# First mixer of a decoder trunk: transposed input, stationary dt weights, running sums spread through device memory

## The chip, the cores and the metric

One core of a Trainium2 chip runs the whole program. The metric is the device time of one launch in microseconds (us). A core has a matrix engine (PE, with its weight loads as PEld), a vector engine (DVE), a scalar engine (ACT), GpSimd (POOL) and a sync engine (SP) that here issues the transfers; 16 DMA engines move the data. Everything is float32.

## The reference

The trunk has two layers: a Mamba-2 layer (here the first mixer, `mixer_a`) with a mixture of experts behind it, and a sliding-window attention layer with a second mixture of experts. The change touches the first mixer only:

```
proj = rms_norm(h, norm_w) @ in_w                      # h: 256 tokens x 1024
z, xbc, dt, q_mem = split(proj)                        # xbc: 2560 channels, dt: 24 heads
xbc = silu(causal_depthwise_conv(xbc, conv_w, conv_b)) # width 4
dt  = softplus(dt + dt_bias); a = -exp(a_log)
# per chunk of 128 tokens:
acum  = cumsum(dt * a)                                 # running sums, one row per head
decay = exp(where(causal, acum[l] - acum[s], -inf))
y = ((C B^T) * decay) @ (x * dt) + (C @ state) * exp(acum) + d_skip * x
y = group_rms_norm(y * silu(z)) * gnorm_w
out = concat(y, memory_cross_attention(q_mem)) @ out_w
```

`decay` needs, for each of 24 heads and 2 chunks, the running sum as a row over l, the same on all 128 partitions, minus the running sum as a column over s.

## The kernel before

All tensors lie with 128 partitions. The work of the mixer is cut into units of PE; each writes one of eight PSUM banks in turn. One list, `order` in `mixer_a`, sets the order of the units, and PE, ACT and DVE each walk the same list: PE makes the unit's matmuls, ACT or DVE evict it and do what follows. So each engine meets the units in the same order, and an engine that waits at one unit holds up everything of its own behind it. PE needs a bank to be freed before it writes it (`U.wait_free`).

The units around the change: `xT` 0 to 3 are transposes of the normed input (ACT evicts them into `xnT`, scaled with `a_norm`), `dt` is the projection to 24 heads, `conv` 0 to 19 are the projections to the 2560 channels (8 matmuls of 128x256 each), whose four taps DVE adds up (L1027, L1029) and ACT passes through silu (L774). DVE makes softplus of dt in a chain of 17 small operations at its place behind `dt`. Then `z`, transposes of xs and B (`xtok`, `bt`), the cumulated sums as columns (`ac`), the norm and transposes of the memory tokens (`memT`).

Then come eight steps (2 chunks times 4 groups), which I number 0 to 7, with a ninth round, 8, for the last products. Step i holds `cb` i (scores C B^T), the two units `A` 2i and 2i+1 (L923: for three heads each, PE multiplies a head's column of dt*a, spread over 128 columns, with the triangle `tri`, which leaves the running sum as a row on all partitions), some units of the memory attention (`between`: `q`, `mk`, `mv`, `sc`, `pT`, `pv`), then `st` or `yo` and `yd` of step i-1. At `A`, DVE subtracts the column (L1053) into the buffer `E[i % 4]`, ACT takes exp (L799), and DVE multiplies with the scores (`decay_scores`, one `A` unit late). `yd` of step i multiplies `E` with x*dt; only after it may `E` be written again, two steps later.

SP issues all transfers on one queue in the order in which they are needed: the input x in two halves, the table `small` (constants and small weights), the weight tiles of the mixer (2 MB each, in two halves of 1 MB, in 11 slots of their own, each refilled when its tile is used), then the first 17 MB of expert weights into slots as they come free. The expert stages behind the mixer use the same slots.

Of the kernel before, what the change touches and what calls it, by code (L numbers as in the profile page):

```python
# [22 lines left out]
F32 = mybir.dt.float32  # L23
# [24 lines left out]
NEG = -1e30  # L48
GRAN = 2048
# [563 lines left out]
def mixer_a(c):  # L613
# [5 lines left out]
             "out_tile mem1_dve " + Router.SEMS)  # L619
    s = c.sems("mixer", names)  # L620
    ld_small = c.sem("ld_small")
    ld_x, ld_mem = ([c.sem(f"ld_{n}{t}") for t in range(NT)] for n in ("x", "mem"))
    with ctx:
# [13 lines left out]
        cbm = [sb(f"cbm{i}", P) for i in range(2)]  # L637
        xw = [acc[:, i * GW:(i + 1) * GW] for i in range(2)]
        sq = xw

# [27 lines left out]

        def freed(kind, i):
# [13 lines left out]
        U = Units(c, order, freed, holds)  # L683
# [18 lines left out]
        x_norm = Norm(c, c.h, 0, s["x_act"], s["x_dve"])  # L702
# [1255 lines left out]
```

## Time and profile before

| | us |
|---|---|
| median of 3 runs | 1407.54 (1406.74 to 1410.73) |
| profiled execution | 1409.6 |
| its span, first to last instruction | 1407.8 |
| PE busy in the span | 1217.6 (86%) |
| DVE, ACT, POOL busy | 271.9, 205.7, 33.5 |
| moved by DMA | 458.76 MB, mean 326 GB/s |

The span is 1.8 us shorter than the profiled execution, and that is 2.1 us above the median. The profile cuts the span in 40 slices of 35.2 us; the mixer takes the first eight, the experts of the first layer come next.

### The profile page before, as it was taken

The numbers are of one execution on the slowest core, as the hardware profiler recorded it, in microseconds if no ns is written. First come the engines' busy times: TensorE is split into PE (matmuls) and PEld (weight loads), VectorE is DVE, ScalarE is ACT, GpSimd is POOL, SyncE is SP. The second block draws the span as 40 slices with busy tenths as digits, with TensorE's granted clock in tenths as the row PEclk, the third lists the DMA queues.
The fourth block names the chain that finished last, engine by engine and source line by source line (L and its number), as shares of the span: only waits on it lengthen the run. The fifth ranks groups of instructions, "written<-read, shape, count | busy, mean of one in ns | idle before, by whom it ended". The sixth has DMA issues, their size and how long they took to land. (4 is left out here: it accounts for less than half of the span.)

```text
span 1407.8 us, 15101 instructions
## 1 busy us (share of the span) xinstructions
PE 1217.6 (86%) x6038; PEld 616.4 (44%) x6038; DVE 271.9 (19%) x679; ACT 205.7 (15%) x490; POOL 33.5 (2%) x42
## 2 busy tenths in 40 slices
PE   6999999989999999659666998989999999657654
PEld 6875875444444445223212566454444444212211
DVE  3541552131111110000001156031101101000001
ACT  3124232110000000000002146130000000000001
POOL 0001210000000000000000011000000000000000
PEclk9999999989999999889887999989999999887877
DMA  9543307559999998999999612549999999999993
GB/s 381 192 144 120 120 0 288 198 234 424 422 423 424 423 424 329 426 420 427 423 425 357 262 60 91 209 139 420 422 423 425 425 424 424 426 423 427 423 424 163
DMA packets 94665, 458.76 MB, mean 326 GB/s; under 512 B 7040, under 2 KB 7040, under 8 KB 61696
## 3 DMA queue, kind: packets, MB, share of 16 engines
q1 hardware_dynamic: 94592, 457.75, 79.7%
q8 instruction: 51, 0.84, 0.2%
q14 instruction: 22, 0.18, 0.0%
HBM read 456.67 MB, written 1.05 MB: 325 GB/s over the span
## 5 line engine op out<-in xcount | busy, mean ns | idle before, releaser
L1395 PE MATMUL bank<-own,e_xg 128*64 128x512 f32 (+1 forms) x1312 | 280.2, 667 | 40.2 <-DMA own<-in_w_up 18.3
L1395 PE MATMUL bank<-late,e_xg 128*64 128x512 f32 (+1 forms) x736 | 177.3, 652 | 35.1 <-DMA own<-in_w_up 19.9
L1404 PE MATMUL bank<-own,e_turned 128*32 128x512 f32 (+1 forms) x656 | 145.9, 704 | 49.2 <-DMA own<-in_w_down 35.6
L1395 PEld LDWEIGHTS bank<-own,e_xg 128*64 128x64 f32 (+1 forms) x1312 | 81.1, 134 | 198.8 <-issue 198.5
L1287 DVE TENSOR_TENSOR e_hid<-e_silu,bank 128x512 f32<-128x512 f32 x24 | 16.5, 688 | 509.7 <-ACT e_silu L1338 509.7
L1395 PEld LDWEIGHTS bank<-late,e_xg 128*64 128x64 f32 (+1 forms) x736 | 50.6, 132 | 129.3 <-issue 129.3
L1370 PEld LDWEIGHTS bank<-e_pick,xs 128*128 128x128 f32 x768 | 94.4, 201 | 20.5 <-issue 18.2
L1370 PE MATMUL bank<-e_pick,xs 128*128 128x128 f32 x768 | 100.9, 288 | 2.1 <-DVE e_pick L1234 2.1
L1404 PE MATMUL bank<-late,e_turned 128*64 128x512 f32 (+1 forms) x368 | 87.5, 673 | 16.7 <-DMA own<-in_w_down 6.3
L1404 PEld LDWEIGHTS bank<-own,e_turned 128*32 128x32 f32 (+1 forms) x656 | 41.0, 139 | 128.0 <-issue 118.4
L1338 ACT ACTIVATE e_silu<-bank 128x512 f32<-128x512 f32 x24 | 14.3, 597 | 548.1 <-PE bank L1395 548.1
L1387 PE MATMUL bank<-e_y,e_gates_T 128*128 128x512 f32 x192 | 86.5, 593 | 1.4 <-ACT e_gates_T L1346 1.4
L394 PE MATMUL bank<-a_xnT,own 128*128 128x256 f32 x384 | 85.3, 384 | 0.0
L394 PEld LDWEIGHTS bank<-a_xnT,own 128*128 128x128 f32 x384 | 73.9, 193 | 10.2
L1292 DVE COPY e_y<-bank 128x512 f32<-128x512 f32 x24 | 16.6, 692 | 256.6 <-PE bank L1404 256.6
L1387 PEld LDWEIGHTS bank<-e_y,e_gates_T 128*128 128x128 f32 x192 | 34.6, 190 | 36.3 <-issue 34.4
L1404 PEld LDWEIGHTS bank<-late,e_turned 128*64 128x64 f32 (+1 forms) x368 | 24.5, 137 | 58.8 <-issue 50.8
L1344 ACT ACTIVATE e_y<-bank 128x512 f32<-128x512 f32 x24 | 14.3, 597 | 244.9 <-PE bank L1404 244.9
L1245 DVE TENSOR_TENSOR e_xg<-bank,small 128x512 f32<-128x512 f32 x48 | 33.2, 692 | 57.8 <-PE bank L1370 57.8
L394 PE MATMUL bank<-own,a_xnT 128*128 128x512 f32 x96 | 42.1, 593 | 0.0
L377 PE MATMUL bank<-own,a_xbcT 128*128 128x512 f32 x96 | 41.8, 593 | 0.0
L394 PE MATMUL bank<-own,b_xnT 128*128 128x512 f32 x64 | 30.6, 636 | 1.1 <-ACT b_xnT L1616 1.1
(326 smaller groups left out, 997.9 us busy)
## 6 DMA issues: line engine op xcount, KB each, us to landing
own<-in_w_up SPq DMA_DIRECT2D x83, 1024.0 KB, 12.0
own<-in_w_down SPq DMA_DIRECT2D x82, 1024.0 KB, 12.5
own<-in_w_gate SPq DMA_DIRECT2D x81, 1024.0 KB, 13.3
late<-in_w_gate SPq DMA_DIRECT2D x47, 1024.0 KB, 13.8
late<-in_w_down SPq DMA_DIRECT2D x46, 1024.0 KB, 12.2
late<-in_w_up SPq DMA_DIRECT2D x45, 1024.0 KB, 11.9
own<-in_a_in_w SPq DMA_DIRECT2D x18, 1024.0 KB, 11.8
own<-in_mem_w_kv SPq DMA_DIRECT2D x8, 1024.0 KB, 9.4
```

The lines of the kernel that those rows point to most:

```text
L377: ins = pe.matmul(U.bank(("out", 2 * t + half))[:, :], src(t, 4 * (m - n) + j), c.rows_at(m, j)[:, 512 * half:512 * half + 512], start=Fal ...
L394: ins = pe.matmul(out, lhsT(k), rhs(k), start=(k == 0), stop=(k == n - 1))
L1245: dve.tensor_tensor(cut(self.xg[:, 512 * half:512 * half + 512], k=4), cut(bank, k=4), spread_last(c.f(f"ffn_norm{layer}", 4 * half, 4 * h ...
L1287: dve.tensor_tensor(self.hid[:, :], self.silu[:, :], self.b_up[:, :], ALU.mult).then_inc(s["hid_ready"], 1)
L1292: dve.tensor_copy(self.y[1][:, :], self.b_down[1][:, :]).then_inc(s["y_ready"], 1)
L1338: act.activation(self.silu[:, :], self.b_gate[:, :], ACT.Silu).then_inc(s["silu_done"], 1)
L1344: act.activation(self.y[0][:, :], self.b_down[0][:, :], ACT.Copy).then_inc(s["y_ready"], 1)
L1370: ins = pe.matmul(bank[:, k * P:(k + 1) * P], xs[:, t, 4 * half + k, :], cut(self.pick, t=NT)[:, t, :], start=(t == 0), stop=(t == NT - 1))
L1387: ins = pe.matmul(self.sums[2 * t + out][:, :], self.gates_T[:, t * P:(t + 1) * P], self.y[out][:, :], start=first, stop=last, skip_group_ ...
L1395: ins = pe.matmul(bank[q * T:(q + 1) * T, :], self.xg[:, at:at + T], cut(tile(q), k=4)[:, k, :], start=(half == 0 and k == 0), stop=(half ...
L1404: ins = pe.matmul(self.b_down[out][q * T:(q + 1) * T, :], self.turned[:, at:at + T], cut(tile(q), j=2)[:, j, 512 * out:512 * out + 512], s ...
```

## The change

- The host also passes x transposed, as `xT` (128 x 2048). SP loads the first 564 columns of `small` (`FIRST_FIELDS`), the halves of `xT` and of weight tile 0 in turn, the rest of `small`, tiles 1 to 4, the memory tokens, and only then x itself.
- The `xT` units are gone. ACT scales `xT` with `a_norm` into `xTw`, DVE squares it, and a new unit `ss` (8 matmuls with `ones` as weights) leaves the sum of squares of each token on all partitions. `norm_x` turns that into `rb`, 1 over the norm, and `xnT` = `xTw` * `rb`.
- `conv` 0 to 3 multiply with the unnormed `xTw`; DVE multiplies their result with `rb` into `raw` before the taps, so they take 5 DVE operations and not 4.
- `dt` is split: `dtp` has the dt weights stationary, 32 columns, in four column groups of the array; ACT copies it to `dtT`; `dt` adds the four groups with two matmuls.
- The `A` units have no PE work. A new unit `acT` makes the running sums as 48 rows, ACT copies them and stores them in device memory (`acum_rows`), and `load_decays` on ACT loads each buffer `E` with three rows broadcast to 128 partitions: for steps 0 and 1 behind `memT`, for step i+2 when PE has done `yd` of step i.

```diff
-        order = [("xT", i) for i in range(4)] + [("dt", 0)]
-        order += [("conv", j) for j in range(NCONV)]
-        order += [("z", 0), ("xtok", 0), ("xtok", 1), ("xtok", 2), ("bt", 0), ("ac", 0), ("z", 1), ("xtok", 3), ("xtok", 4), ("xtok", 5)]
+        order = [("conv", 0), ("conv", 1), ("ss", 0), ("conv", 2), ("conv", 3), ("dtp", 0), ("conv", 4), ("dt", 0)]
+        order += [("conv", j) for j in range(5, NCONV)]
+        order += [("z", 0), ("xtok", 0), ("xtok", 1), ("xtok", 2), ("bt", 0), ("ac", 0), ("acT", 0), ("z", 1), ("xtok", 3), ("xtok", 4), ("xtok", 5)]
...
         @block.sync
         def _(sp):
-            for t in range(NT):
-                sp.dma_start(cut(c.h, t=NT)[:, t, :], g["x"][0, t * P:(t + 1) * P, :]).then_inc(ld_x[t], 16)
-            sp.dma_start(c.small[:, :], g["small"]).then_inc(ld_small, 16)
-            for n in range(2):
+            sp.dma_start(c.small[:, 0:FIRST_SMALL], g["small"][:, 0:FIRST_SMALL]).then_inc(ld_first, 16)
+            for half in range(2):
+                at = slice(4 * half * SEQ, 4 * (half + 1) * SEQ)
+                sp.dma_start(xT[:, at], g["xT"][:, at]).then_inc(ld_xT[half], 16)
+                c.load_mixer_half(sp, 0, half)
+            sp.dma_start(c.small[:, FIRST_SMALL:], g["small"][:, FIRST_SMALL:]).then_inc(ld_small, 16)
+            for n in range(1, 5):
                 c.load_mixer_tile(sp, n)
...
+            for k in range(KD):
+                act.wait_ge(ld_xT[k // 4], 16)
+                act.activation(cut(xTw, k=KD)[:, k, :], cut(xT, k=KD)[:, k, :], ACT.Copy, scale=c.f("a_norm", k, k + 1)).then_inc(s["xw_ev"], 1)
+            act.wait_ge(s["rb_dve"], 1)
+            act.activation(rb[:, :], rb[:, :], ACT.Sqrt).then_inc(s["rb_act"], 1)
+
+            def load_decays(st):
+                for i in (2 * st, 2 * st + 1):
+                    ch, gr = steps[st]
+                    row = SSD_HEADS * ch + HG * gr + 3 * (i % 2)
+                    rows = acum_rows[row:row + 3, :].rearrange("(o r) l -> o (r l)", o=1)
+                    act.dma_start(E[i % 4][:, :], rows.broadcast_to([P, GW])).then_inc(e_loaded[i % 4], 16)
...
+                if kind == "dtp":
+                    U.wait_done(act, key)
+                    act.activation(dtT, bank[:, 0:SEQ], ACT.Copy).then_inc(s["dtp_ev"], 1)
+                    act.wait_ge(ld_small, 16)
+                elif kind == "acT":
+                    U.wait_done(act, key)
+                    act.activation(acT, bank[0:NT * SSD_HEADS, 0:P], ACT.Copy).then_inc(s["acT_ev"], 1)
+                    act.wait_ge(s["acT_ev"], 1)
+                    act.dma_start(acum_rows, acT).then_inc(s["acum_stored"], 16)
...
+                    if i == 3:
+                        act.wait_ge(s["acum_stored"], 16)
+                        for st in range(2):
+                            load_decays(st)
...
+                elif kind == "yd" and i < 6:
+                    U.wait_done(act, key)
+                    load_decays(i + 2)
...
+                elif kind == "ss":
+                    pe.wait_ge(s["sq_dve"], 2)
+                    project(c, pe, out[:, 0:256], lambda k: c.f("ones"), lambda k: cut(squares, k=KD)[:, k, :])
...
+                elif kind == "dtp":
+                    pe.wait_ge(s["xn_dve"], 2)
+                    for k in range(KD):
+                        q = DT_ROWS * (k % 4)
+                        ins = pe.matmul(out[q:q + DT_ROWS, 0:SEQ], cut(c.f("dt_w"), k=KD)[:, k, :], cut(xnT, k=KD)[:, k, :],
+                                        start=(k < 4), stop=(k >= 4))
+                    ins.then_inc(c.units_done, 1)
                 elif kind == "dt":
-                    pe.wait_ge(s["xT_ev"], 8)
+                    pe.wait_ge(s["dtp_ev"], 1)
...
+                elif kind == "acT":
+                    pe.matmul(out[0:NT * SSD_HEADS, 0:P], adt[:, :], c.f("tri"), start=True, stop=True).then_inc(c.units_done, 1)
-                elif kind == "A":
-                    ch, gr = steps[i // 2]
-                    for hh in range(3):
-                        hd = HG * gr + 3 * (i % 2) + hh
-                        ins = pe.matmul(out[:, hh * P:(hh + 1) * P], cut(adt, t=NT)[:, ch, hd:hd + 1].broadcast_to([P, P]),
-                                        c.f("tri"), start=True, stop=True)
-                    ins.then_inc(c.units_done, 1)
...
+            def norm_x():
+                U.wait_done(dve, ("ss", 0))
+                dve.tensor_scalar(rb[:, :], U.bank(("ss", 0))[:, 0:SEQ], 1.0 / D, EPS, ALU.mult, ALU.add).then_inc(s["rb_dve"], 1)
+                dve.wait_ge(s["rb_act"], 1)
+                dve.reciprocal(rb[:, :], rb[:, :]).then_inc(s["rb_dve"], 1)
+                dve.wait_ge(s["rb_dve"], 2)
+                dve.wait_ge(s["xw_ev"], KD)
+                for half in range(2):
+                    k = slice(4 * half, 4 * half + 4)
+                    dve.tensor_tensor(cut(xnT, k=KD)[:, k, :], cut(xTw[:, :], k=KD)[:, k, :], spread_mid(rb[:, :], 4), ALU.mult).then_inc(s["xn_dve"], 1)
...
+                    if i < 4:
+                        step(dve.tensor_tensor(raw[i], bank[:, 0:SEQ], rb[:, :], ALU.mult))
+                        bank = raw[i]
...
-                    U.wait_done(dve, key)
-                    if i >= 4:
-                        dve.wait_ge(c.units_done, U.at["yd", (i - 4) // 2] + 1)
+                    dve.wait_ge(e_loaded[i % 4], 16 * (i // 4 + 1))
```

How the instructions stand, in three places. First PE's queue from the start to the first z unit, before (`xs` is the normed input, `own` a weight slot):

```order
L333 MATMUL bank<-small,xs 128x128 x16
L885 MATMUL bank<-small,a_xnT 128x24 x16
L394 MATMUL bank<-a_xnT,own 128x256 x160
L394 MATMUL bank<-own,a_xnT 128x512 x8
L333 MATMUL bank<-small,a_xbcT 128x128 x16
```

and after (`xs` now holds `xTw`; L936 is `dtp`, L942 is `dt`):

```order
L922 MATMUL bank<-xs,own 128x256 x8
L396 MATMUL bank<-xs,own 128x256 x8
L396 MATMUL bank<-a_xbcT,small 128x256 x8
L396 MATMUL bank<-xs,own 128x256 x16
L936 MATMUL bank<-a_xnT,small 32x256 x8
L396 MATMUL bank<-a_xnT,own 128x256 x8
L942 MATMUL bank<-small,a_xbcT 128x24 x2
L396 MATMUL bank<-a_xnT,own 128x256 x120
```

The transposes and the 16 dt matmuls ahead of the projections are gone; five conv units, `ss` and `dtp` stand ahead of `dt`, and fifteen conv units stand behind it.

Second, ACT's queue at the same place, before (L766 evicts the transposes, L770 is the exp of dt, L774 the silu of the conv units):

```order
L766 ACTIVATE a_xnT<-bank,small 128x256 x8
L770 ACT_TABLE_LOAD
L770 ACTIVATE a_dt<-a_dt 128x48
L771 ACTIVATE a_ea<-small 128x24
L774 ACT_TABLE_LOAD
L774 ACTIVATE a_xbcT<-a_acc 128x256 x20
```

and after, with what each waits for (L815 is now the silu, L790 the copy of `dtp` to `dtT`, L811 the exp of dt):

```order
L756 ACTIVATE xs<-memT,small 128x256 [waits ld_xT0] x4
L756 ACTIVATE xs<-memT,small 128x256 [waits ld_xT1] x4
L758 ACTIVATE a_cbm<-a_cbm 128x256 [waits mixer_rb_dve]
L815 ACT_TABLE_LOAD
L815 ACTIVATE a_xbcT<-a_acc 128x256 [waits mixer_conv_dve] x4
L790 ACTIVATE a_xbcT<-bank 128x256 [waits units_done]
L815 ACTIVATE a_xbcT<-a_acc 128x256 [waits mixer_conv_dve,ld_small]
L811 ACT_TABLE_LOAD
L811 ACTIVATE a_dt<-a_dt 128x48 [waits mixer_dt_dve]
```

The copy L790 stands behind the silu of conv 0 to 3, and each of those waits for DVE.

Third, PE in step 7, before (L917 is `cb`, L923 the two `A` units, L394 is `mk` 1, L349 `pv` 0, L341 `sc` 1, L943 `yo`, L949 `yd` 6):

```order
L917 MATMUL bank<-a_xbcT 128x128
L923 MATMUL bank<-small,a_dt 128x128 x6
L394 MATMUL bank<-late,own 128x256 x8
L349 MATMUL bank<-a_xbcT,late 128x256 x2
L341 MATMUL bank<-late,a_qT 128x256 x2
L943 MATMUL bank<-a_xbcT 128x384
L949 MATMUL bank<-late,xs 128x64 x6
```

and ACT from there on after the change (L767 are the two loads for step 7, behind `yd` 5; L840 the exps of `A` 14 and 15; L834 the eviction of `mk` 1, L856 that of `pv` 0, L848 the exps of `sc` 1):

```order
L767 DMA xs<-acum_rows 128x384 [waits units_done]
L767 DMA xs<-acum_rows 128x384
L840 ACTIVATE xs<-xs 128x384 [waits mixer_seg_dve] x2
L834 ACTIVATE late<-bank 128x256 [waits units_done]
L856 ACTIVATE a_qT<-bank 128x256 [waits units_done]
L848 ACTIVATE a_xbcT,a_smc<-bank,a_smc 128x256 [waits mixer_sm_max,units_done]
```

PE's row L923 is gone from each of the eight steps, and two transfers stand on ACT ahead of the exps of steps 2 to 7.

## Rows read from the trace of the kernel before

**Rows 1.** The page: busy share of the DMA engines, in tenths, 40 slices.

```profile
DMA  9543307559999998999999612549999999999993
```

**Rows 2.** Waits of PE, 0 to 240 us: total, times, longest.

```profile
PE bank L333 <- DVE xs L422: 10.9, 1, 10.9
```

**Rows 3.** Waits of PE, 290 to 700 us, the longest group.

```profile
PE bank L1404 <- DMA own<-in_w_down: 19.9, 4, 6.3
```

**Rows 4.** Timeline of the start: start us, length, what, count, idle and releaser.

```profile
0.75 0.87 SPq L712 DMA_DIRECT2D h<-in_x  x2
...
4.63 1.06 ACT L412 ACTIVATE xs<-h 128x1024 f32<-128x1024 f32 x1 [2.60 <-DMA h<-in_x]
...
8.45 0.88 POOL L468 TENSOR_TENSOR small<-small 128x288 f32<-128x288 f32 x1 [8.00 <-DMA small<-in_small]
...
10.87 3.65 PE L333 MATMUL bank<-small,xs 128*128 128x128 f32 x16 [10.87 <-DVE xs L422]
...
15.44 7.02 PE L885 MATMUL bank<-small,a_xnT 128*128 128x24 f32 x32 [0.93 <-ACT a_xnT L766]
...
22.29 37.94 PE L394 MATMUL bank<-a_xnT,own 128*128 128x256 f32 x167
```

**Rows 5.** Timeline of PE: the first z unit, behind conv 19.

```profile
93.09 7.03 PE L394 MATMUL bank<-own,a_xnT 128*128 128x512 f32 x16
```

**Rows 6.** Timeline of DVE and ACT: conv 0 and the start of conv 1.

```profile
27.75 0.54 DVE L1027 TENSOR_SCALAR a_acc<-bank,small 128x256 f32<-128x256 f32 x1 [0.51 <-PE bank L394]
28.33 1.52 DVE L1029 SCALAR_TENSOR_TENSOR a_acc<-bank,small,a_acc 128x255 f32<-128x255 f32 x3
29.88 0.42 ACT L774 ACTIVATE a_xbcT<-a_acc 128x256 f32<-128x256 f32 x1 [5.24 <-DVE a_acc L1029]
31.20 0.54 DVE L1027 TENSOR_SCALAR a_acc<-bank,small 128x256 f32<-128x256 f32 x1 [1.36 <-PE bank L394]
```

**Rows 7.** DVE operations of other widths: a timeline row, then groups by form.

```profile
23.67 0.45 DVE L1010 RECIPROCAL a_dt<-a_dt 128x48 f32<-128x48 f32 x1
...
L1089 DVE TENSOR_TENSOR late<-late,xs 128x384 f32<-128x384 f32 x8 | 4.5, 558 | 0.3
L1073 DVE TENSOR_TENSOR a_xbcT<-a_xbcT,a_smc 128x512 f32<-128x512 f32 x4 | 2.8, 692 | 0.1
L997 DVE TENSOR_SCALAR late<-late,a_gss 128x384 f32<-128x384 f32 x8 | 2.7, 416 | 0.0
```

**Rows 8.** Timeline of PE around the A units of step 0.

```profile
133.12 1.50 PE L923 MATMUL bank<-small,a_dt 128*128 128x128 f32 x12
134.46 7.03 PE L394 MATMUL bank<-own,a_xnT 128*128 128x512 f32 x16
```

**Rows 9.** Timeline of PE around a wait in the experts (32-column weights, four column groups).

```profile
562.51 3.64 PE L1404 MATMUL bank<-own,e_turned 128*32 128x512 f32 x32 [0.47 <-ACT e_turned L1341]
572.16 5.12 PE L1404 MATMUL bank<-own,e_turned 128*32 128x512 f32 x32 [6.01 <-DMA own<-in_w_down]
```

**Rows 10.** Windows there: length, busy (count) of PE, PEld, DVE, ACT, POOL, PEclk, DMA share, GB/s.

```profile
568.00:570.00 2.00, 0.00 (x0) 0.00 (x0) 0.00 (x0) 0.00 (x0) 0.00 (x0) 0.59 1.03 424
...
574.00:576.00 2.00, 2.00 (x20) 0.55 (x16) 0.00 (x0) 0.00 (x0) 0.00 (x0) 0.70 1.08 451
576.00:578.00 2.00, 2.00 (x19) 0.93 (x12) 0.66 (x1) 0.66 (x2) 0.00 (x0) 1.00 0.96 397
```

**Rows 11.** Step 7, from the timelines of PE, DVE and ACT: yd 5; A 14; eviction of mk 1; sc 1.

```profile
193.58 1.45 PE L949 MATMUL bank<-late,xs 128*128 128x64 f32 x12
...
197.11 0.86 DVE L1053 TENSOR_SCALAR xs<-bank,a_acum 128x128 f32<-128x128 f32 x3
...
200.14 0.38 ACT L793 ACTIVATE late<-bank 128x256 f32<-128x256 f32 x1
...
200.80 1.03 PE L341 MATMUL bank<-late,a_qT 128*128 128x256 f32 x4
```

**Rows 12.** Line L248 (SP's 1 MB loads), 60 to 80 us: issue to landing.

```profile
DMA to landing us min/median/max: 4.7/5.9/7.4
```

**Rows 13.** Line L394 of PE, 23 to 24 us: count, busy, mean ns.

```profile
L394 PE MATMUL bank<-a_xnT,own 128*128 128x256 f32 x4 | 2.1, 669 | 0.0
```

More of the change, by code:

```diff
@@ L636, in mixer_a @@
         yt = c.xs[:, 4 * GW:5 * GW]
[L637 removed]
+        cbm2 = sb("cbm", 2 * P)
+        cbm = [cbm2[:, P * i:P * i + P] for i in range(2)]
         xw = [acc[:, i * GW:(i + 1) * GW] for i in range(2)]
         sq = xw
+        xT, xTw, rb = c.memT1, c.xs, cbm2
+        squares, raw, dtT = xbcT[:, 8 * SEQ:16 * SEQ], [xbcT[:, (16 + i) * SEQ:(17 + i) * SEQ] for i in range(4)], xbcT[:, 15 * SEQ:16 * SEQ]
+        acT = qT[0:NT * SSD_HEADS, 0:P]
         state, ex, pTs = xbcT[:, 0:4 * GW], [xbcT[:, 4 * GW + 512 * i:4 * GW + 512 * i + 512] for i in range(2)], xbcT[:, 4 * GW + 1024:4 * GW + 1536]
@@ L681, in freed @@
                     "out": (s["h_new"], i + 1)}[kind]
-        U = Units(c, order, freed, holds)
+        pe_order = [key for key in order if key[0] != "A"]
+        U = Units(c, pe_order, freed, holds)
         R = Router(c, U, s, 0, xnT, acc)
@@ L717, in _ @@
                 sp.dma_start(cut(mem, t=NT)[:, t, :], g["mem"][0, t * P:(t + 1) * P, :]).then_inc(ld_mem[t], 16)
-            for n in range(2, TILES_A):
+            for t in range(NT):
+                sp.dma_start(cut(c.h, t=NT)[:, t, :], g["x"][0, t * P:(t + 1) * P, :]).then_inc(ld_x[t], 16)
+            for n in range(5, TILES_A):
                 for half in range(2):
@@ L733, in _ @@
         def _(act):
-            for t in range(NT):
-                act.wait_ge(ld_x[t], 16)
-                x_norm.act(act, t)
+            act.wait_ge(ld_first, 16)
+            act.activation(c.norm_r[:, 6:7], c.f("ones", 0, 1), ACT.Sqrt)
+            for k in range(KD):
[9 more added lines that the diff above has]
+                    act.dma_start(E[i % 4][:, :], rows.broadcast_to([P, GW])).then_inc(e_loaded[i % 4], 16)
             for key in order:
@@ L863, in _ @@
         def _(pe):
-            for key in order:
+            pe.wait_ge(ld_first, 16)
+            for key in pe_order:
                 kind, i = key
@@ L871, in _ @@
                     U.wait_free(pe, key)
-                if kind == "xT":
-                    if i == 0:
-                        pe.wait_ge(ld_small, 16)
-                        pe.wait_ge(s["x_dve"], 6)
-                    norm_T_units(c, pe, out, i)
+                if key == ("conv", 0):
+                    for k in range(KD):
+                        if k % 4 == 0:
+                            c.wait_job(pe, ("mixer", 0, k // 4))
+                        pe.wait_ge(s["xw_ev"], k + 1)
+                        ins = pe.matmul(out[:, 0:256], c.cols_at(0, k)[:, 0:P], cut(xTw, k=KD)[:, k, :], start=(k == 0), stop=(k == KD - 1))
+                    ins.then_inc(c.units_done, 1)
+                elif kind == "ss":
+                    pe.wait_ge(s["sq_dve"], 2)
+                    project(c, pe, out[:, 0:256], lambda k: c.f("ones"), lambda k: cut(squares, k=KD)[:, k, :])
                 elif kind == "memT":
@@ L972, in chain @@
                 return step
-            for t in range(NT):
-                x_norm.dve(dve, t)
+            for half in range(2):
+                at = slice(4 * half * SEQ, 4 * (half + 1) * SEQ)
+                dve.wait_ge(ld_xT[half], 16)
+                dve.tensor_tensor(squares[:, at], xT[:, at], xT[:, at], ALU.mult).then_inc(s["sq_dve"], 1)
+            dve.wait_ge(ld_first, 16)
+            def norm_x():
[5 more added lines that the diff above has]
+                dve.wait_ge(s["xw_ev"], KD)
+                for half in range(2):
+                    k = slice(4 * half, 4 * half + 4)
+                    dve.tensor_tensor(cut(xnT, k=KD)[:, k, :], cut(xTw[:, :], k=KD)[:, k, :], spread_mid(rb[:, :], 4), ALU.mult).then_inc(s["xn_dve"], 1)
+            norm_x()
             y_step = chain(s["y_dve"])
@@ L1021, in _ @@
                 elif kind == "conv":
-                    step = chain(s["conv_dve"], 4 * i)
+                    step = chain(s["conv_dve"], conv_done(i))
                     U.wait_done(dve, key)
+                    if i == 4:
+                        dve.wait_ge(ld_small, 16)
                     if i >= 3:
```

69 lines of the change are left out of this document (39 added, 30 removed).

## The prediction

> **What bounds the kernel now.** I read the page's slices first. The DMA engines are at 8 or 9 tenths from the tenth slice on, but for five slices in the middle; in the eight slices of the mixer they are at 9, 5, 4, 3, 3, 0, 7 and 5 [rows 1]. So the experts are bound by their weights, the mixer is not. The waits of PE come next. In the first 240 us PE waits once for long, 10.9 us at the very start, for the normed input [rows 2]; from there it works without a gap to the router. Later the waits are for weights, such as 19.9 us for w_down in 290 to 700 us [rows 3]. A stage bound by PE and one bound by DMA behind it add up: the stream of expert weights cannot run ahead of the mixer, because the 17 slots hold it. So each us that the mixer gets shorter should come off the time whole, and I work out only by how much PE reaches its router sooner. What ends last there is PE's own queue, and it is walked strictly in order.
>
> **Start of the projections.** Before, PE starts at 10.87 us, runs 16 transposes and the dt matmuls, and reaches conv 0 at 22.29 [rows 4] and the first z unit at 93.09 [rows 5]. A conv unit takes 3.45 us at full pace (27.75 to 31.20 [rows 6]); 20 of them are 69.1 us of the 70.8. The other 1.7 us are matmuls at half pace: mean 669 ns and four in 23 to 24 us [rows 13].
>
> When do the new inputs land? Two halves of x and `small` (2.11 MB) are there at 8.45 us, the first half of x (0.52 MB) at 4.63 [rows 4]: a stream of 0.41 MB/us that starts at 3.3 us. The new order gives: first table 4.0, `xT` half 5.3, weights half 7.8, second `xT` 9.1, second weights 11.7. ACT scales a quarter of a half in about 0.42 us (the 128x256 activation [rows 6]) and is ready before each half of the weights.
>
> Conv 0 then starts at 7.9. Its first eight instructions run at half pace, 3.4 us, the rest at 11.75. After the pause in the experts the granted clock was 0.50 to 575.2 us (0.70 in 574 to 576) and 1.00 from there, 3.0 us after the restart at 572.16 [rows 9, 10], so I take 1.2 GHz to 11 and 2.4 GHz behind: conv 0 ends at 13.5 (15.2 if all of it is slow). Conv 1 ends at 17.0, `ss` at 20.4, conv 2 and 3 at 27.3. `dtp`: 32 instructions with 32-column weights and 512 columns take 3.64 us [rows 9], so 16 with 256 columns take 0.9; end 28.2. Conv 4 ends at 31.6. [...]
>
> **The new wait.** `dt` needs ACT's copy of `dtp`, which stands on ACT behind the silu of conv 0 to 3, and these wait for DVE. DVE begins when `ss` is done, 20.8 with 0.4 of latency: 0.54 (the 256-wide operation [rows 6]); ACT's root 0.42; the reciprocal of 256, from 0.45 for 48 [rows 7] with 0.15 of it taken as fixed and the rest scaled, 1.75 (bounds 1.2, and 2.4 if all of it scales); two multiplications of 1024, from 0.56 for 384 and 0.69 for 512 [rows 7], 1.22 each. With gaps that is 26.1. Then four conv units: 0.43 for the new multiplication (between 0.3 and 0.56), 0.35 for the first tap, which now reads SBUF (2.7 us for eight of 384 [rows 7], bound 0.54), 1.52 for the rest, 0.1 of gaps: 2.4 each, 35.7. Silu and copy 0.42 each: `dt` on PE at 36.6, where PE has stood since 31.6. Behind it on PE stand all fifteen conv units. `dt` takes 0.45, the fifteen 51.8, and the clock will have dropped in these 5 us: in the experts' pause of 6.0 us the clock was 0.59 in the window that begins 1.9 us into it, and came back 3.0 us after the restart [rows 9, 10]. That costs 1.6 us. The z unit starts at 37.05 + 51.8 + 1.6 = 90.5 and not 93.1: **-2.6 us**. The head start of 9 us is mostly given back. Bounds: -4.7 (DVE 0.5 sooner, clock kept) and +1 (all of conv 0 slow, first tap 0.54, reciprocal 2.4). DVE then catches up, at 2.1 us a unit against 3.45 [rows 6]. The dt chain of 17 operations hides as before.
>
> **The A units.** From 133.12 to 134.46 PE spends 1.34 us on them [rows 8], eight times: -10.7. `acT` is one such matmul of 128 columns, +0.2. **-10.5 us**. Its copy and store on ACT, the first four loads and their landing lie ahead of step 0 by two z units of 7.03 us each [rows 5] and cost nothing; with that cover gone they would cost one landing.
>
> **The new transfers.** From step 2 on a load may be issued only when `yd` of two steps before is done, at time T on PE. The row of PE's own unit is replaced by: ACT sees the end and issues (0.3), landing L. For L the nearest row is 4.7 us for 1 MB [rows 12], of which 2.6 are its bytes at 0.41 MB/us: 2.1 fixed, plus 0.5 for 0.2 MB, plus 0.6 for sharing with a weight tile that SP loads just then: 3.3 from the issue (bounds 2.5 and the row's own maximum, 7.4). Behind the waiting operation on DVE stand three subtractions (0.86 [rows 11]) and the multiplication with the scores (0.55), which PE's `yd` needs: ready at T + 0.3 + L + 1.4. PE has `cb` 0.27, the units between and 0.64 for `st` to do meanwhile. With one 3.45 us unit between (steps 2 and 4) it is there at T + 4.4 and stands 0.6 us each time; with seven us between (3, 5, 6) it never waits. Step 7 is worse. There `sc` 1 needs `mk` 1 evicted, and ACT does that behind the exps of A 14 and 15. Before: T = 193.58 + 1.29 = 194.87; DVE starts A 14 at 197.11, `mk` 1 is evicted at 200.52, `sc` 1 starts at 200.80 [rows 11]. So the path through DVE and ACT is 5.65 us long and hides PE's A units already. Without them PE comes to `sc` 1 at T + 4.6, and the path, begun at T + 0.3 + L = T + 3.6 and 3.4 long, ends at T + 7.0: 2.4 us. Together 3.6, with 0.4 for the weight tile that is in flight at step 2: **+4.0 us** (bounds 1.7 at L = 2.5, 12 at L = 6).
>
> ACT also waits at each `yd` now. What stands behind that are exps, which could not run sooner either, since their buffer is only free then.
>
> By the Trainium skill (DMA: Bandwidth & Descriptors, Anatomy of one DMA) such a transfer takes 2.0 us and bytes / 436e9, an estimate of 2.45 here; no run here shows one of this size yet. With it the stalls would sum to about 1.6 and the time to some 1396. It also says (Issuing engines are not separate DMA queues) that ACT's transfers interleave with SP's on the same 16 engines, which speaks against the change.
>
> **Sum.** -2.6 - 10.5 + 4.0 = -9.1 us. The profiled span of 1407.8 would become 1398.7, and the median of 1407.5 becomes 1398.4. The profiled execution lies 2.1 above the median, within the spread of 4 us of the three runs.
>
> **Rivals.**
> (a) More gain, under 1394. DVE needs less for the SBUF operations, so `dt` comes by 35 and the wait is short enough for the clock, and loads land in 2.5 us: -4.7 - 10.5 + 1.7 = -13.5, 1394. Against it: both must hold.
> (b) The transfers eat the gain. Stalls by L: steps 2 and 4 L - 2.7 each, step 7 L - 0.9, steps 3, 5, 6 from about 6.2, 7.1 and 6.7. At L = 5 they sum to 8.7, at 6 to 11.7: 1403 to 1406. For it: the tile in flight at steps 2 and 4, and a median of 5.9 us for loads that come in pairs [rows 12]. Against it: ACT's load is a fifth of such a one in bytes.
> (c) Slower. The same mechanism in steps 2 to 7: it loses from L = 6.4 (stalls 13.1) and by more than 4.2 us from L = 7.3. That is so when the broadcast of one row to 128 partitions, or a queue behind SP's tiles, makes the landing as late as 7.4 [rows 12]. Then 2 x 4.7 + 6.5 + 1.2 + 0.3 + 0.7 = 18.1, less 13.1: +5, 1412.5.
> (d) The head start is lost altogether: conv 0 slow throughout and DVE at its upper bounds, +1 for the start. That alone gives 1402.
>
> **Chances.** The forecast, with (d) in it, 1394 to 1403.3: 0.68. (a) 0.11. (b) 0.16. (c) 0.05. A difference of 0.3%, 4.2 us, is about what a measurement of this kernel can tell from none. Faster by more than that: 0.68 + 0.11 = 0.79; within it 0.16, slower 0.05. For the range I go down to 1392.5, half of (a), and up to 1405, part of (b).
>
> **What would show it.** PE's conv 0 in two pieces, from 7.9 and 11.75. A wait of PE for ACT's copy (L790) of about 5 us, with the clock at half for some 3 us behind it. The z unit at 90.5. No long PE wait at steps 3, 5, 6; about 0.6 at 2 and 4, and 2.4 at `sc` 1. ACT's loads landing in some 3.3 us. The router reached 9 us sooner and the rest shifted whole. It would be wrong if the loads take 5 us or more, if DVE's start path is shorter than 26.1 or if the DMA-bound part does not shift along.

## The result and the profile after

The changed kernel takes 1415.84 us (median of 6 runs, 1415.0 to 1418.34) against 1407.6 (6 runs, 1405.24 to 1410.73) before: a ratio of 1.0059, 95% interval 1.0044 to 1.0074. It is slower by 8 us where I forecast 9 us faster. The profiled execution took 1415.68 us with a span of 1413.8, against 1407.8.

The page's rows of the DMA engines come first, as in [rows 1]; under each row of shares stands the row of GB/s. After:

```profile
DMA  9643408569999999999998612559999999999994
GB/s 357 243 145 142 164 23 330 197 247 418 418 417 416 415 416 367 422 409 421 414 418 339 237 60 90 208 191 417 416 417 418 417 418 415 420 415 421 414 418 168
```

and before:

```profile
GB/s 381 192 144 120 120 0 288 198 234 424 422 423 424 423 424 329 426 420 427 423 425 357 262 60 91 209 139 420 422 423 425 425 424 424 426 423 427 423 424 163
```

The shares say the same in both kernels, 9 tenths wherever the experts stream their weights. The GB/s don't: 420 to 425 before in most of those slices, 414 to 418 after. Equally busy engines moved 1.6% less. This is in code that the diff doesn't touch. My rows had the shares alone, and these can't show it.

Waits of PE in 0 to 240 us after, which answer to [rows 2], with total, times and longest:

```profile
PE bank L922 <- DMA own<-in_a_in_w: 9.5, 2, 9.3
PE bank L942 <- ACT a_xbcT L790: 4.1, 1, 4.1
PE bank L1002 <- issue: 3.6, 2, 3.4
PE bank L343 <- ACT late L834: 1.2, 1, 1.2
```

The first is the start (10.9 before). The others are the three new stalls: `dt` for the copy of `dtp`, `yd` of step 3, and `sc` 1 for the eviction of `mk` 1.

Timeline of PE at the start, which answers to [rows 4, 5]:

```profile
9.28 3.75 PE L922 MATMUL bank<-xs,own 128*128 128x256 f32 x8 [9.28 <-DMA own<-in_a_in_w]
13.22 2.22 PE L922 MATMUL bank<-xs,own 128*128 128x256 f32 x8 [0.19 <-DMA own<-in_a_in_w]
...
29.18 1.07 PE L936 MATMUL bank<-a_xnT,small 128*32 128x256 f32 x16
30.18 3.72 PE L396 MATMUL bank<-a_xnT,own 128*128 128x256 f32 x16
38.03 1.04 PE L942 MATMUL bank<-small,a_xbcT 128*128 128x24 f32 x4 [4.13 <-ACT a_xbcT L790]
38.91 54.77 PE L396 MATMUL bank<-a_xnT,own 128*128 128x256 f32 x240
...
93.51 7.03 PE L396 MATMUL bank<-own,a_xnT 128*128 128x512 f32 x16
```

Both halves of conv 0 wait for weights; `dt` starts at 38.03 after a wait of 4.13 us; the first z unit is at 93.51, no sooner than the 93.09 of [rows 5].

Steps 3 and 4, timelines of PE, ACT's queue and DVE (L767 are the two loads for step 4, L1127 the subtraction on `A` 8, L1052 the product for `A` 7, L1002 `yd` 3):

```profile
160.00 0.88 SPq L250 DMA_DIRECT2D own<-in_a_out_w  x2
...
161.93 0.82 ACTq L767 DMA_DIRECT2D xs<-acum_rows  x2
...
168.39 0.68 DVE L1127 TENSOR_SCALAR xs<-xs,a_acum 128x128 f32<-128x128 f32 x3 [4.98 <-DMA xs<-acum_rows]
168.99 0.55 DVE L1052 TENSOR_TENSOR xs<-xs,a_cbm 128x384 f32<-128x384 f32 x1
...
169.64 1.80 PE L1002 MATMUL bank<-late,xs 128*128 128x64 f32 x12 [3.37 <-issue]
...
171.76 8.22 PE L396 MATMUL bank<-own,late 128*128 128x512 f32 x16
```

Two weight halves were issued by SP at 160.00, and the loads at 161.93 land behind them: DVE gets `A` 8 at 168.39. PE stands at `yd` 3 because DVE makes the product of `A` 7 only behind the subtraction on `A` 8. Then `mv` 0 takes 8.22 us and not 7.03. The landings of all 16 loads, minimum, median and maximum:

```profile
DMA to landing us min/median/max: 2.9/3.3/6.4
```

Step 7, which answers to [rows 11]:

```profile
195.86 1.03 PE L351 MATMUL bank<-a_xbcT,late 128*128 128x256 f32 x4
198.10 1.10 PE L343 MATMUL bank<-late,a_qT 128*128 128x256 f32 x4 [1.22 <-ACT late L834]
```

PE has four milestones in every one of these kernels: the first z unit, the gather of the router's picks, the first expert matmul, the end of the span. The last two columns were read from the program, not the trace: where slot 0 of the weight slots (`own`) starts in SBUF in each partition, and what is left of that over a multiple of 256 bytes.

| kernel | z | gather | experts | span | experts to end | GB/s, 1000 to 1200 us | start of `own` | over 256 |
|---|---|---|---|---|---|---|---|---|
| before | 93.09 | 289.92 | 296.23 | 1407.8 | 1111.6 | 424 | 42240 | 0 |
| after | 93.51 | 287.31 | 292.44 | 1413.8 | 1121.4 | 417 | 42592 | 96 |
| e5_aligned | 92.47 | 287.84 | 293.31 | 1404.9 | 1111.6 | 423 | 42752 | 0 |
| e6_shifted | 91.46 | 288.30 | 294.86 | 1417.5 | 1122.6 | 417 | 42592 | 96 |
| e9_off128 | 91.26 | 288.11 | 294.69 | 1417.7 | 1123.0 | 417 | 42368 | 128 |
| e10_off32 | 91.26 | 288.10 | 294.79 | 1420.5 | 1125.7 | 416 | 42272 | 32 |
| e3_start_only | 92.89 | 289.74 | 296.15 | 1418.5 | 1122.4 | 416 to 417 | 42592 | 96 |
| e4_sp_queue | 93.94 | 283.03 | 288.88 | 1411.1 | 1122.2 | 417 | 42592 | 96 |
| e7_start_aligned | 92.01 | 288.86 | 295.53 | 1404.6 | 1109.1 | 424 | 42752 | 0 |
| e11_copy_early | 85.97 | 282.80 | 288.73 | 1400.2 | 1111.5 | 424 | 42752 | 0 |
| e12_act_moves | 85.06 | 277.73 | 283.37 | 1397.5 | 1114.1 | 424 | 42752 | 0 |
| e8_best | 86.02 | 274.44 | 279.60 | 1391.0 | 1111.4 | 424 | 42752 | 0 |

Each slot is 8192 bytes in a partition, 32 times 256, so all 17 slots share the remainder in the last column. From the first expert matmul to the end the changed kernel takes 9.8 us more than before, and that is its whole loss: it gets there 3.8 us sooner.

### The profile page after: what moved, and what is told of

It reads as the page before. It is cut to its first block and busy times, and to the rows that moved or that the text cites. A ratio compares the mean times of both kernels' runs of the same rounds, so it can differ in the third digit from the quotient of the medians.

```text
span 1413.8 us, 14909 instructions
## 1 busy us (share of the span) xinstructions
PE 1213.5 (86%) x5932; PEld 600.7 (42%) x5932; DVE 272.5 (19%) x683; ACT 203.5 (14%) x488; POOL 32.7 (2%) x42
## 5 line engine op out<-in xcount | busy, mean ns | idle before, releaser
L1469 PE MATMUL bank<-own,e_xg 128*64 128x512 f32 (+1 forms) x1312 | 283.1, 674 | 36.3 <-DMA own<-in_w_up 16.8
L1478 PE MATMUL bank<-late,e_turned 128*64 128x512 f32 (+1 forms) x368 | 91.3, 696 | 19.9 <-DMA own<-in_w_down 11.0
L396 PE MATMUL bank<-a_xnT,own 128*128 128x256 f32 x320 | 72.8, 390 | 0.0
L396 PEld LDWEIGHTS bank<-a_xnT,own 128*128 128x128 f32 x320 | 62.4, 196 | 9.2 <-issue 0.4
```

The lines of the kernel that those rows point to most:

```text
L396: ins = pe.matmul(out, lhsT(k), rhs(k), start=(k == 0), stop=(k == n - 1))
L1469: ins = pe.matmul(bank[q * T:(q + 1) * T, :], self.xg[:, at:at + T], cut(tile(q), k=4)[:, k, :], start=(half == 0 and k == 0), stop=(half ...
L1478: ins = pe.matmul(self.b_down[out][q * T:(q + 1) * T, :], self.turned[:, at:at + T], cut(tile(q), j=2)[:, j, 512 * out:512 * out + 512], s ...
```

## Experiments: is it the queue or the tensors?

My first two suspects for the slower stream were parts of the change that last beyond the mixer: a second engine's DMA queue in use, and the new tensors. Each was put alone into the kernel before.

**e1_act_ring.** ScalarE issues one transfer of 4 KB.

```diff
+            act.dma_start(spare[:, :], g["small"][:, 0:8]).then_inc(extra, 16)
+            act.wait_ge(extra, 16)
```

> The kernel before, and one transfer of 4 KB issued by ACT at the very start. Nothing else is changed. In the changed kernel the weight stream of the experts ran at 416 to 418 GB/s and not at 423 to 425, in the whole expert stages. If a second transfer queue (ACT's) is what slows it (theory R), the stream falls to about 417 GB/s here too and the time rises by 8 to 12 us. If the layout of the tensors in device memory does it (theory T), the stream stays at 424 and the time within 2 us of before.

Measured 1409.76 us (10 runs), ratio 1.0008 (0.9995 to 1.002). The stream stays at 422 to 424 GB/s. The use of ACT's queue isn't it.

**e2_tensors.** The kernel before also loads `xT` and stores 48 rows to `acum_rows`, both by SP.

```diff
+            sp.dma_start(c.memT1[:, :], g["xT"]).then_inc(ld_xT, 16)
+            sp.dma_start(acum_rows, c.small[0:NT * SSD_HEADS, 0:P]).then_inc(stored_rows, 16)
```

> The kernel before, with the two tensors of the change in device memory: xT is loaded once (into the tile of the transposed memory tokens, which is overwritten later), and 48 rows are stored to acum_rows, both by SP; ACT issues nothing. Theory T: the stream falls to about 417 GB/s, time +8 to +12 us. Theory R: 424 GB/s and within 2 us of before.

Measured 1408.6 us (10 runs), ratio 1.0005 (0.9994 to 1.0017), stream 422 to 424 GB/s. Nor are the tensors in device memory.

**e3_start_only.** The changed kernel with the `A` units back on PE and without the transfers of running sums.

```diff
-        order += [..., ("ac", 0), ("acT", 0), ("z", 1), ...]
+        order += [..., ("ac", 0), ("z", 1), ...]
+                elif kind == "A":
...
-                    dve.wait_ge(e_loaded[i % 4], 16 * (i // 4 + 1))
+                    U.wait_done(dve, key)
```

> The changed kernel with the A units back on PE: no store, no loads by ACT, no acum_rows, but xT, the new start and dtp as changed. From the two traces the start alone gives the first z unit at 93.5 and not 93.1 us, so the mixer would be 0.4 us longer than before. Theory R: stream 424 GB/s, time 1408 (+0.4). Theory T, if xT does it: stream 417, time 1416 to 1420. If acum_rows does it: 424 as by R.

Measured 1419.52 us, ratio 1.007 (1.0053 to 1.0087), stream 416 to 417 GB/s: slower even than the changed kernel, with no transfer of its own left on ACT. So the loss is there without the running sums, and it isn't at the start either: z is at 92.89 and the gather at 289.74, both as before.

**e4_sp_queue.** The changed kernel with store and loads issued by SP, each at a fixed place in the list of weight tiles.

```diff
-                elif kind == "yd" and i < 6:
-                    U.wait_done(act, key)
-                    load_decays(i + 2)
...
+                for st in {(12, 1): (0,), (13, 1): (1, 2), (14, 1): (3, 4, 5)}.get((n, half), ()):
+                    sp.wait_ge(c.units_done, U.at["yd", st] + 1)
+                    load_decays(st + 2)
```

> The changed kernel with the store and the 16 loads issued by SP in place of ACT, and the weight tiles that were in flight at steps 2 and 4 issued behind them. Theory R: stream 424 GB/s, so the mixer's gain is left over: time 1402 to 1405. Theory T: stream 417, time 1412 to 1414. In either case PE's wait of 3.4 us in step 4 shrinks to under 1 us if it was the weight tile in flight that delayed the load, and the clock does not fall there.

Measured 1411.45 us (10 runs), ratio 1.0027 (1.0016 to 1.0038). The waits of PE in the mixer:

```profile
PE bank L925 <- DMA own<-in_a_in_w: 9.3, 2, 9.1
PE bank L945 <- ACT a_xbcT L802: 4.1, 1, 4.1
PE bank L343 <- ACT late L840: 1.3, 1, 1.3
PE bank L1005 <- issue: 0.5, 2, 0.3
```

The wait at `yd` falls from 3.6 to 0.5 us and half pace behind it goes. From z to the gather the kernel takes 189.09 us, after 193.80, before 196.83. The stream is still at 417 GB/s. The queue of the loads costs 4.4 us in the times, and the stream's loss is something else.

## Experiments: the place of the weights in SBUF

What the three kernels at 416 to 417 GB/s so far (the changed one, e3_start_only, e4_sp_queue) share is the table `small`, 8672 bytes per partition and not 8320. It stands ahead of the weight slots in SBUF and moves all of them: `own` starts at 42592, 96 bytes past a multiple of 256, and not at 42240, which is a multiple.

**e5_aligned.** The changed kernel and 40 unused columns in `small`, which bring `own` to 42752, a multiple of 256 again.

```diff
 FIRST_SMALL = sum(w for _, w in FIRST_FIELDS)
+FIELDS += [("pad", 40)]
```

> The changed kernel with 40 unused columns added to the table small, so that the weight slots behind it in SBUF start at a multiple of 256 bytes again (42752), as in the kernel before (42240); in the changed kernel they start at 42592, 96 bytes past one. Theory A (alignment of the weights' destination): the stream of expert weights returns to 424 GB/s and the 3.8 us by which the experts start sooner are left: 1403 to 1406. Theory S (something else in the new start, as the order or the split of the first transfers): stream 417, time 1415 to 1417.

**e6_shifted.** The kernel before and 88 unused columns, which put `own` exactly where the change puts it. Nothing else is changed.

```diff
-          ("dt_w", KD * SSD_HEADS)]
+          ("dt_w", KD * SSD_HEADS), ("pad", 88)]
```

> The kernel before with 88 unused columns added to small, which moves the slots by the same 352 bytes as the change does and changes nothing else but 45 KB more to load. Theory A: stream 417 GB/s, 1415 to 1420. Theory S: 424 GB/s, within 1.5 us of before.

e5_aligned takes 1405.45 us (9 runs), ratio 0.9975 (0.9964 to 0.9986); e6_shifted 1419.8 (6 runs), ratio 1.0077 (1.006 to 1.0094). Each way the step is 10 to 12 us. The stream in 1000 to 1200 us, first of the kernel before, then after, then e5_aligned, then e6_shifted:

```profile
DMA packets 14931, 84.77 MB, mean 424 GB/s; under 512 B 1293, under 2 KB 1293, under 8 KB 7891
```

```profile
DMA packets 14574, 83.44 MB, mean 417 GB/s; under 512 B 1268, under 2 KB 1268, under 8 KB 7527
```

```profile
DMA packets 15051, 84.67 MB, mean 423 GB/s; under 512 B 1291, under 2 KB 1291, under 8 KB 8156
```

```profile
DMA packets 14460, 83.49 MB, mean 417 GB/s; under 512 B 1271, under 2 KB 1271, under 8 KB 7282
```

The packets are of much the same size in all four, 5.6 to 5.8 KB on average; some 1.5% fewer bytes arrive in 200 us. Unused columns alone bring the loss and take it away, so it comes from where the length of `small` puts what lies behind it. Two things stay unseparated. The padding moves every tensor behind `small` in SBUF, the small ones too, though nearly all bytes of this stretch go into the weight slots. And it makes the table larger in device memory, so that the weights may start elsewhere there. No run moved the slots alone. Against the second: e2_tensors adds two tensors in device memory and stays at 424 GB/s in this stretch, and with `acum_rows` or without it the stream is at 417 (the changed kernel, e3_start_only) and at 423 to 424 (e5_aligned, e7_start_aligned).

**e9_off128 and e10_off32.** As e6_shifted with 32 and with 8 columns: 128 and 32 bytes past a multiple of 256.

```diff
-          ("dt_w", KD * SSD_HEADS)]
+          ("dt_w", KD * SSD_HEADS), ("pad", 32)]
```

```diff
-          ("dt_w", KD * SSD_HEADS)]
+          ("dt_w", KD * SSD_HEADS), ("pad", 8)]
```

> The kernel before with 32 unused columns more in the tile of small constants, so that every weight slot in SBUF starts 128 bytes past a multiple of 256 (own at 42368) instead of at one. Theory A in its first form (any start that is not a multiple of 256 costs): experts' stream 416 to 418 GB/s, 1417 to 1420 us. Theory A in its second form (only a start that is not a multiple of 128, or of 64, costs): 423 to 425 GB/s, 1406 to 1410 us. Rival (the number of columns or the size of the constants' load costs, not the address): in between, growing with the columns, about 1412.

> The kernel before with 8 unused columns more, so that every weight slot starts 32 bytes past a multiple of 256 (own at 42272). First form (any start that is not a multiple of 256 costs): 416 to 418 GB/s, 1417 to 1420 us. If only the distance counts, 32 bytes cost a third of what 96 do: about 1411. If 32 bytes is a fine start too: 423 to 425 GB/s, 1406 to 1410 us.

Measured 1419.98 us, ratio 1.0079 (1.0063 to 1.0094), at 417 GB/s, and 1423.0 us, ratio 1.0103 (1.0085 to 1.0121), at 416. So the first form holds at every distance tried: 32, 96 and 128 bytes cost 11 to 14 us. The number of columns doesn't decide it (8 cost the most), and the loss doesn't grow with the distance. The 1423.0 lies above the 1417 to 1420 of that form. All four runs at 32 bytes are slower than all four at 128 (1421.02 at least against 1420.79 at most), but the intervals of the ratios overlap, and why 32 should cost more stays open. 64 bytes wasn't tried, and both good starts, 42240 and 42752, are an odd multiple of 256; an even one wasn't tried either.

The Trainium skill (DMA: Bandwidth & Descriptors, How a descriptor splits into AXI transactions) says that a transaction has to start at a multiple of 256 bytes and that a descriptor that doesn't start at one fetches unused bytes from the boundary below. It says so of reading; that the same holds on the written side, here SBUF, is my extension of it. By that rule, the traces agree in sign and in that every remainder tried costs. An estimate from it is too high: with 83.44 MB in 14574 packets, 5.7 KB each, and a packet taken for a descriptor, one transaction more on 22 would be 4.5%, and the traces show 1.6%.

**e7_start_aligned.** e3_start_only with the 40 columns: what the new start is worth alone.

```diff
+FIELDS += [("pad", 40)]
```

> The new start alone (A units on PE, no transfers through device memory), with the slots at a multiple of 256 bytes. The start alone brought the first z unit to 92.9 us against 93.1. Theory A: 424 GB/s, 1407 to 1409. Theory S: 417, 1417 to 1420 as without the padding (1419.5).

Measured 1408.78 us (12 runs), ratio 0.9998 (0.9987 to 1.0008). The new start alone gives nothing. e5_aligned, with the running sums through device memory as well, is 3.3 us faster than this one.

## Experiments: the waits that were left

**e11_copy_early.** e7_start_aligned, and ACT copies `dtp` behind silu of conv 1.

```diff
+            act_order = [key for key in order if key not in (("dtp", 0),)]
+            act_order.insert(act_order.index(("conv", 1)) + 1, ("dtp", 0))
-            for key in order:
+            for key in act_order:
```

> The aligned kernel with the new start only (the e7 build: start changed, running sums still on TensorE) and one move on ScalarE: the copy of dt's projection goes behind silu of conv unit 1 instead of standing behind every conv unit. Theory: the 4.1 us wait of TensorE for that copy goes, and with it the 1.7 us by which the first in_z unit was slow behind it: 1408.8 less 6, 1402 to 1404 us, the first in_z unit at about 86 to 88. Rival (the wait passes to the next one late, the conv units or the own weights): 1406 to 1409.

Measured 1400.96 us (5 runs), ratio 0.9944 (0.993 to 0.9957). PE at the start, first of e7_start_aligned, then of e11_copy_early:

```profile
37.04 1.05 PE L920 MATMUL bank<-small,a_xbcT 128*128 128x24 f32 x4 [4.12 <-ACT a_xbcT L780]
37.91 54.26 PE L397 MATMUL bank<-a_xnT,own 128*128 128x256 f32 x240
...
92.01 4.46 PE L397 MATMUL bank<-own,a_xnT 128*128 128x512 f32 x10
```

```profile
33.72 0.52 PE L922 MATMUL bank<-small,a_xbcT 128*128 128x24 f32 x4
...
85.97 7.03 PE L397 MATMUL bank<-own,a_xnT 128*128 128x512 f32 x16
```

The wait is gone, not passed on, and `dt` takes half the time. The first z unit starts at 85.97, 6.0 us sooner, as expected; the median fell by 7.8, to 1400.96, which is 1 us below the lower end of the 1402 to 1404 expected. The start that gives nothing as the change has it (e7_start_aligned) is worth 7 to 8 us once one copy on ACT stands two units earlier.

**e12_act_moves.** e5_aligned with that move and with the eviction of `mk` 1 between the exps of `A` 14 and 15.

```diff
+            act_order = [key for key in order if key not in (("dtp", 0), ("mk", 1))]
+            act_order.insert(act_order.index(("conv", 1)) + 1, ("dtp", 0))
+            act_order.insert(act_order.index(("A", 14)) + 1, ("mk", 1))
```

> The changed kernel, aligned (the e5 build), with both moves on ScalarE (copy of dt's projection behind silu of conv unit 1; eviction of mask unit 1 between the exponentials of A14 and A15), the row stores and spread loads still on ScalarE's queue. By the sum 1405.5 less 4.1 and 1.7 (copy wait and half pace) less 1.2 (TensorE's wait for sc1): 1398 to 1399 us. It differs from e8 (1392.9) in the queue of the transfers alone: the theory that the loads on ScalarE's queue land late at step 4 puts 3 to 6 us between them, the rival (the queue is nothing, all of e8's gain is the moves) puts this one at 1393 to 1394.

**e8_best.** e4_sp_queue with the 40 columns and both moves. It differs from e12_act_moves in the queue of the transfers alone.

```diff
+FIELDS += [("pad", 40)]
...
+            act_order.insert(act_order.index(("conv", 1)) + 1, ("dtp", 0))
+            act_order.insert(act_order.index(("A", 14)) + 1, ("mk", 1))
```

> The changed kernel with slots at a multiple of 256 bytes, store and loads of the running sums issued by SP ahead of the weight tiles, and two moves in ACT's own order: the copy of dtp directly behind the silu of conv 1, and the eviction of mk 1 between the exps of A 14 and 15. Theory: PE's wait of 4.1 us for the copy and the half pace behind it (about 1.7) go, and the wait of 1.2 at sc 1. With theory A that is 1407.6 - 6.5 - 5.8 - 1.2 = 1394. If the copy is early but PE then waits for something later in the start (the taps on DVE, banks), the first z unit stays at 93 and the time at 1400. With theory S it would be 10 us more in either case.

e12_act_moves takes 1397.44 us (5 runs), ratio 0.9913 (0.9899 to 0.9927), 0.6 us under what was expected, and e8_best 1392.85 (5 runs), ratio 0.9885 (0.9869 to 0.99), 1.1 under. Waits of PE in the mixer of e12_act_moves and, below, of e8_best:

```profile
PE bank L1006 <- issue: 3.5, 2, 3.3
...
PE bank L344 <- ACT late L838: 0.2, 1, 0.2
```

```profile
PE bank L929 <- DMA own<-in_a_in_w: 8.6, 1, 8.6
PE bank L1009 <- issue: 1.0, 2, 0.7
PE bank L344 <- ACT late L844: 0.2, 1, 0.2
```

The move of `mk` 1 takes PE's wait at `sc` 1 from 1.2 to 0.2 us. The wait at `yd` 3 stays as long as the loads are on ACT's queue and goes to 0.7 on SP's, where no weight half is ahead of them. Of the 4.6 us between the medians, the milestones place 4.7 between the first z unit and the experts (198.31 against 193.58). The spans differ by more, 6.5 us, of which 2.7 are in the experts' stage, where the aligned kernels lie between 1109.1 and 1114.1 without a cause that I could name. e8_best is the version to keep: 15 us under the kernel before, 23 under the changed one.

## Why the prediction was wrong

| term | predicted | measured in the profiled spans |
|---|---|---|
| first z unit | -2.6 | +0.4 |
| z unit to gather | -6.5 (-10.5 and +4.0) | -3.0 |
| gather to experts | 0 | -1.2 |
| experts to end | 0 | +9.8 |
| sum | -9.1 | +6.0 |

**The last row is the step that failed.** "The rest shifted whole" took for granted that the experts' stage costs the same in both kernels. As to when it starts, that holds: before, e5_aligned and e8_best reach the experts at 296.23, 293.31 and 279.60 and then take 1111.6, 1111.6 and 1111.4. But the change made the table of constants longer, the weight slots moved by 352 bytes, and the stream into them fell from 424 to 417 GB/s. With the slots put back, the changed kernel takes 1405.45, which is faster than before by 2.8 us; its span of 1404.9 lies 6.2 above my sum of 1398.7, and this is what the next rows add up to (2.0 at the first z unit, 5.0 up to the gather, 0.8 back at the gather). None of my rivals had the place in SBUF. It was to be seen in the diff, where `small` gets new fields; the price was not, since no kernel with other slots had been run.

**The start: right mechanisms, sizes too small.** The halves of the weights came at 9.28 and 13.22 us where I had 7.9 and 11.75. Only part of that is the place in SBUF, as e7_start_aligned starts at 8.65 and 12.46 and e5_aligned at 8.99. DVE's first conv operation came at 27.44 (26.1), and from there the chain went as worked out:

```profile
23.38 1.75 DVE L1039 RECIPROCAL a_cbm<-a_cbm 128x256 f32<-128x256 f32 x1 [0.48 <-ACT a_cbm L758]
...
27.44 0.42 DVE L1101 TENSOR_TENSOR a_xbcT<-bank,a_cbm 128x256 f32<-128x256 f32 x1
27.90 0.41 DVE L1103 TENSOR_SCALAR a_acc<-a_xbcT,small 128x256 f32<-128x256 f32 x1
28.34 1.52 DVE L1105 SCALAR_TENSOR_TENSOR a_acc<-a_xbcT,small,a_acc 128x255 f32<-128x255 f32 x3
```

The reciprocal took the 1.75 us that I had scaled from [rows 7], and a conv unit 2.47 against 2.4. `dt` started at 38.03 (36.6), after a wait of 4.1 (5). Then the clock:

```profile
36.00:38.00 2.00, 0.00 (x0) 0.00 (x0) 1.86 (x5) 0.69 (x2) 0.00 (x0) 0.90 1.04 414
38.00:40.00 2.00, 1.97 (x7) 1.79 (x8) 1.74 (x5) 0.49 (x2) 0.00 (x0) 0.50 1.02 406
...
42.00:44.00 2.00, 2.00 (x6) 1.61 (x5) 1.76 (x8) 0.88 (x1) 0.00 (x0) 0.50 1.03 383
44.00:46.00 2.00, 2.00 (x9) 1.73 (x9) 1.75 (x8) 0.00 (x0) 0.00 (x0) 0.89 1.06 391
```

(length, busy of PE, PEld, DVE, ACT and POOL, PEclk, DMA share, GB/s). It was still granted for most of the pause, fell to 0.50 just as PE went on, and rose only in 44 to 46, after some 6 us of work and not 3. The fifteen conv units lost 2.85 us to it where I had 1.6 (93.51 less 38.91 is 54.6, and fifteen at 3.45 are 51.75), and `dt` itself another 0.4. Altogether 1.4 from the start, 1.25 and 0.4 here are the 3.0 us of the first row. One pause of 4 us cost some 7 in all, and rival (d), the head start lost altogether, came nearest to this term in size. Its two conditions weren't met: the second half of conv 0 took 2.22 us, where half pace throughout would be 3.4, and DVE's reciprocal lay at 1.75 and not at the bound of 2.4.

**The A units: right.** Without the stalls the time from step 0 (133.78) to `mk` 2 behind step 7 would be 60.0 us, which is 70.7 before less 10.7. It was 67.2.

**The stalls: 7 us and not 4.** At step 2 PE stood 0.4 us (1.0 forecast), at step 7 1.4 (2.4). Steps 3, 5 and 6 had none, as forecast. At `yd` 3, where the loads for step 4 count, it stood 3.5 instead of 0.6, and half pace behind it cost 1.7. The typical landing of 3.3 us was met to the tenth; what failed is that I put all loads at the typical value, although I knew of a weight tile in flight then. That load took 6.4, and my own formula, L - 2.7, gives 3.7 for it. Rival (b), with 5 to 6 us for every load, was nearer in the sum (8.7 at 5) and no nearer in the split. In e4_sp_queue, where the loads are ahead of the tile on one queue, PE waits 0.2 us there.

The Trainium skill's 2.0 us and bytes / 436e9 (DMA: Bandwidth & Descriptors, Anatomy of one DMA), which that section gives for transfers issued from GpSimd and not from ACT, made an estimate of 2.45 us a load; the trace differs, with 2.9 at least and 3.3 typically. What it says of ACT's transfers sharing the engines with SP's (Issuing engines are not separate DMA queues) the trace bears out, by the 6.4.

**Gather.** The router's gather took 5.20 us and not 6.38, since the clock rose at 290 to 292 instead of 294 to 296. No part of the change is aimed there, and I take it as chance of when the clock rises: among the kernels here it is 5.20 to 6.77.

**The start before was a slow one.** z lies at 93.09 before and at 91.26 to 91.46 in e6, e9 and e10, whose start has the same instructions. The difference is in the products of the `dt` unit behind the transposes. PE in 15 to 17 us, first of the kernel before, then of e6_shifted:

```profile
L885 PE MATMUL bank<-small,a_xnT 128*128 128x24 f32 x8 | 1.9, 390 | 0.9 <-ACT a_xnT L766 0.9
```

```profile
L885 PE MATMUL bank<-small,a_xnT 128*128 128x24 f32 x15 | 1.9, 270 | 0.9 <-ACT a_xnT L766 0.9
```

In e6 they begin at full pace. Then, with PE at work without a gap, the granted clock falls; windows of e6_shifted, columns as in [rows 10]:

```profile
15.00:17.00 2.00, 1.61 (x15) 1.61 (x15) 0.00 (x0) 1.62 (x2) 0.00 (x0) 1.00 1.04 385
18.00:20.00 2.00, 2.00 (x11) 2.00 (x11) 0.00 (x0) 0.00 (x0) 0.00 (x0) 0.50 1.05 408
24.00:26.00 2.00, 2.00 (x9) 1.67 (x9) 0.96 (x5) 0.00 (x0) 0.00 (x0) 0.87 1.04 384
```

Before, these products go at half pace from their first to their last, 7.02 us for the unit against 4.94 (the PEclk of its trace reads 1.00 there, so this is told by the matmuls' durations alone). e2, e9 and e10 are like e6; e1 is like before. So my 93.09 was one draw of two, and against the other draw the new start is 2 us late and not 0.4. Which draw an execution gets, no run here explains. Milestones of single profiles are good to some 2 us for this reason.

## What to carry to other kernels

When a change adds, widens or drops a tensor in SBUF, look at where everything behind it comes to lie, above all the slots of a DMA-bound stream, and pad it to a multiple of 256 bytes: 8 stray columns cost this kernel 14 us. Compare GB/s between two profiles and not only the busy share, which reads 9 tenths either way. A pause of PE costs more than its length where the clock is lost with it (4.1 us cost some 7 here), so the operation that PE waits for should be first on its engine as soon as its own input is there; and a small urgent load belongs on the queue ahead of the large ones, not beside them.

## What the runs showed of the hardware that was not expected

- Weight slots that start 32, 96 or 128 bytes past a multiple of 256 in a partition are filled at 416 to 417 GB/s, those at a multiple at 423 to 424, with the DMA engines' busy share the same.
- PE's clock after a pause of 4.1 us with work at its full rate before it: granted 0.90 in the window that ends with the pause, 0.50 from 38 to 44 us, back in 44 to 46. In e11_copy_early, with no pause, the granted clock was 1.00 throughout 28 to 44 us.
- After the shorter pause of 3.4 us at `yd` 3 (3.3 in e5_aligned) the loss differed between two builds with the same code: `mv` 0 took 8.22 us in the changed kernel and 8.91 in e5_aligned, 7.03 where no pause is near.
- The granted clock also fell with no pause at all: in e6_shifted, during the `dt` unit's products of 24 columns, from 1.00 in 15 to 17 us to 0.50 in 18 to 20, PE busy throughout, and it was back in 24 to 26. The same instructions took 4.67 to 5.06 us in four builds and 7.02 to 7.03 in two.
- A load that spreads three rows over 128 partitions (192 KB) landed in 2.9 us at best, 3.3 typically, and in 6.4 where two weight halves of 1 MB had been issued 1.9 us ahead of it on another queue.
